# Prompt attention with its query tiles in falling order, and the next pair's projections moved to the short steps

## The reference

```
s = einsum('bqhr,bkr->bhqk', ql_b, ckv) + einsum('bqhd,bkd->bhqk', qr_b, kr)
s = where(pos[None, :] <= qp_b[:, None], s * ATTN_SCALE, NEG_INF)
p = softmax(s, axis=-1)
o = einsum('bhqk,bkr->bqhr', p, ckv)
```

## Time and profile before

| what | us |
|---|---|
| median of three runs | 2076.92 |
| the profiled execution | 2072.72 |
| its span, first to last instruction | 2070.9 |
| PE busy | 1934.8 |
| DVE busy | 1031.0 |
| ACT busy | 643.5 |

### The profile page before, as it was taken

One profiled execution on the slowest core, in us unless ns is written; L12 is line 12 of the kernel. 1 busy time (PEld: TensorE's weight loads), 2 busy tenths in 40 slices (PEclk: granted clock), 3 DMA queues, 4 the chain that ended last, 5 costly groups with the idle time before them and its releaser, 6 DMA issues. The chain is left out here.

```text
span 2070.9 us, 50992 instructions
## 1 busy us (share of the span) xinstructions
PE 1934.8 (93%) x22434; PEld 1248.1 (60%) x22434; DVE 1031.0 (50%) x2399; ACT 643.5 (31%) x1711; POOL 223.2 (11%) x223
## 2 busy tenths in 40 slices
PE   8999989988999999999989999899889999999997
PEld 5665667775566567754446656677755665677443
DVE  2017127775566468833330071277755664688333
ACT  1222234442455432310012222344424554322000
POOL 0000001010000034202100000001100000442022
PEclk9999999997999989999999999999979999999999
DMA  6102010000000367731121020100000002677121
GB/s 213 51 1 91 1 48 4 4 4 23 1 1 10 83 232 270 260 129 61 67 64 51 1 92 0 48 4 4 4 23 1 1 14 79 244 272 266 62 81 53
DMA packets 50112, 151.13 MB, mean 73 GB/s; under 512 B 15138, under 2 KB 19490, under 8 KB 40420
## 3 DMA queue, kind: packets, MB, share of 16 engines
q1 hardware_dynamic: 37604, 72.36, 10.5%
q0 software_dynamic: 12288, 75.51, 9.8%
HBM read 130.27 MB, written 12.86 MB: 69 GB/s over the span
## 5 line engine op out<-in xcount | busy, mean ns | idle before, releaser
L406 PE MATMUL psum<-work 128*128 128x368 f32 x1536 | 484.6, 476 | 8.9 <-DMA work<-w_z 6.6
L406 PEld LDWEIGHTS psum<-work 128*128 128x128 f32 x1536 | 293.6, 192 | 193.7 <-issue 8.2
L2465 PE MATMUL psum<-work,mixed 128*128 128x512 f32 (+1 forms) x576 | 248.8, 592 | 1.6 <-PEq L2137 1.6
L2465 PEld LDWEIGHTS psum<-work,mixed 128*128 128x128 f32 (+1 forms) x576 | 106.2, 186 | 137.7 <-issue 137.7
L2333 DVE STREAM_TRANSPOSE work<-work 128x1024 f32<-128x1024 f32 x128 | 150.5, 1214 | 0.3 <-issue 0.2
L1906 ACT ACTIVATE work<-psum,work 128x128 f32<-128x128 f32 (+8 forms) x130 | 98.0, 754 | 160.6 <-DVE work L2015 160.4
L1786 PE MATMUL psum<-work 96*128 96x512 f32 (+3 forms) x384 | 139.1, 495 | 2.3 <-ACT work L1906 2.1
L2077 POOL DMA_INDIRECT work<-cache_ckv,pages x64 | 60.7, 948 | 606.9 <-PE psum L1740 377.7
L2237 PE MATMUL psum<-work,ckv 128*64 128x256 f32 x1024 | 117.6, 382 | 0.7 <-ACT ckv L2292 0.7
L2513 DVE SCALAR_TENSOR_TENSOR work<-work,psum 128x512 f32<-128x512 f32 (+1 forms) x36 | 23.1, 683 | 162.1 <-PE psum L2465 162.1
L1786 PEld LDWEIGHTS psum<-work 96*128 96x128 f32 x384 | 67.4, 189 | 60.0 <-issue 43.5
(11 more groups left out here) (311 smaller groups left out, 2953.0 us busy)
## 6 DMA issues: line engine op xcount, KB each, us to landing
work<-w_z SPq DMA_DIRECT2D x4, 2560.0 KB, 11.0
work<-w_out SPq DMA_DIRECT2D x4, 2048.0 KB, 8.8
xres<-work SPq DMA_DIRECT2D x16, 512.0 KB, 2.9
work<-xT SPq DMA_DIRECT2D x4, 1104.0 KB, 8.8
work<-x_tok SPq DMA_DIRECT2D x8, 512.0 KB, 4.0
work<-xres SPq DMA_DIRECT2D x8, 512.0 KB, 4.3
work<-w_z SPq DMA_DIRECT2D x1, 2304.0 KB, 13.9
o_ckv<-ckv SPq DMA_DIRECT2D x2, 1104.0 KB, 4.3
```

Of the source, the lines that this page charges most:

```text
L406: return nc.tensor.matmul(zb[i % 2][n][:, 0:G], z_weights(m, g)[:, k, lo:lo + Z_W[i]], xT[:, k, span(n)], start=k == 0, stop=k == DK - 1)
L2465: last = nc.tensor.matmul(yb[t % 2][half][0:n, :], m.mixed[:, k, lo:lo + n], wo[half][:, k, :], start=k == 0, stop=k == DK - 1)
```

## The change

Two tables change; no instruction is added or taken away. `T_ORDER` becomes falling. The eleven pieces of the next pair, which stood in the slots 0 to 6 of a pair (none in slot 2, one in slot 3), now stand in the slots 2 to 7, with one per half slot but for the second half of slot 7. The `norm` pieces of the pair before move from slots 2 and 3 to both halves of slot 1.

```
-T_ORDER = [7, 0, 6, 1, 5, 2, 4, 3]
+T_ORDER = [7, 6, 5, 4, 3, 2, 1, 0]
...
-        PIECES += [(_s, 0, "q", _h, 0), (_s, 1, "q", _h, 1), (_s + 1, 0, "q", _h, 2), (_s + 1, 1, "lat", _h, 0),
...
+        PIECES += [(_s + 2, 0, "q", _h, 0), (_s + 2, 1, "q", _h, 1), (_s + 3, 0, "q", _h, 2),
...
-        PIECES += [(_s + 2, 0, "norm", _p - 1, 0), (_s + 3, 0, "norm", _p - 1, 1)]
+        PIECES += [(_s + 1, 0, "norm", _p - 1, 1), (_s + 1, 1, "norm", _p - 1, 0)]
```

More of the change, by code:

```diff
@@ L1603 @@
     if _p + 1 < PAIRS:
-        PIECES += [(_s, 0, "q", _h, 0), (_s, 1, "q", _h, 1), (_s + 1, 0, "q", _h, 2), (_s + 1, 1, "lat", _h, 0),
-                   (_s + 3, 1, "q", _h + 1, 0), (_s + 4, 0, "q", _h + 1, 1), (_s + 4, 1, "q", _h + 1, 2),
-                   (_s + 5, 0, "lat", _h + 1, 0), (_s + 5, 1, "k", _p + 1, 0), (_s + 6, 0, "k", _p + 1, 1),
-                   (_s + 6, 1, "k", _p + 1, 2)]
+        PIECES += [(_s + 2, 0, "q", _h, 0), (_s + 2, 1, "q", _h, 1), (_s + 3, 0, "q", _h, 2),
+                   (_s + 3, 1, "k", _p + 1, 0), (_s + 4, 0, "lat", _h, 0), (_s + 4, 1, "q", _h + 1, 0),
+                   (_s + 5, 0, "q", _h + 1, 1), (_s + 5, 1, "q", _h + 1, 2), (_s + 6, 0, "k", _p + 1, 1),
+                   (_s + 6, 1, "lat", _h + 1, 0), (_s + 7, 0, "k", _p + 1, 2)]
     if _p >= 1:
-        PIECES += [(_s + 2, 0, "norm", _p - 1, 0), (_s + 3, 0, "norm", _p - 1, 1)]
+        PIECES += [(_s + 1, 0, "norm", _p - 1, 1), (_s + 1, 1, "norm", _p - 1, 0)]
 PIECES += [(FIRST[PAIRS - 1] + 3, 1, "turn8", 0, 0), (N_STEP, 1, "norm", PAIRS - 1, 1),
```

## The result

The changed kernel takes 2087.02 us (median of five runs, 2085.25 to 2090.1), against 2076.92 for the kernel before: a ratio of 1.0038, 95% interval 1.002 to 1.0055. The forecast was 2080.2 with a range of 2074 to 2088. The medians differ by 10.1 us, which alone would be 1.0049; the ratio stands for 7.9 us and its interval for 4 to 11. So the sign of the sum was right and the size was not, since +3.3 was worked out. The measured time lies 1 us inside the upper end of the range.

The account below looks back on a forecast made before the run. PE's work was taken to bound the block, the order deciding only its idle time. Per layer -1.0 + 2 x 0.64 + 1.35 = +1.63, over two layers +3.3, added to the median: 2080.2 us, range 2074 to 2088.

Parts of the forecast that it names:

- +3.3: Both layers together: the forecast change in us, from a sum of waits of +1.63 a layer; bounds 0 and +8.
- What bounds the kernel: Attention block: PE's work is the block, and the order decides only over its idle time, some 5%.
- The interior pair: Interior pairs, twice a layer: new waits of 3.61 us against 2.97 before, +0.64 each.
- What would show it: Trace after: waits at `k`, `lat`, tile 7's, tile 6's and pair 3's first scores; a pair's period about 0.6 longer.
- Pair 0: First pair of a layer: waits of 3.9 us, including 1.2 for late ACT, against 4.9 before, so -1.0.
- Tail step and pair 3: End of a layer's block: waits of 5.05 us, including 2.3 behind the tail step, against 3.7 before, so +1.35.
- the guess for the last three steps: Last three steps, which have no pieces: 0.3 to 0.6 us at each of four handovers, 1.6 in all.
- its own last sign: Whole block: the prediction called itself wrong if the clock leaves 1.00 within the block.
- the one of the clock: Rival, pair 3's entry: the 2.3 us wait brings one clock fall in each layer, +13, 2093 us; chance 0.06.
- DVE did not become the bound: Rival, tiles 3 and 2: DVE becomes the bound, +1.5 us a pair, +9 in all, 2089; chance 0.14.
- That the short steps' waits don't arise: Rival, short steps: DVE and ACT drain pieces in time, -6.5 us a layer, -13 in all, 2064; chance 0.07.
- It does nothing: Rival, whole block: PE's work is the same and waits only change places, sum 0, 2077 us; chance 0.05.

Follow-up runs that it names:

- e1_fill: Changed kernel plus two needless matmuls between the tail step and pair 3's first scores; 2080.06 us, 1.0019 of the kernel before.
- e8_pair2_old_order: Changed kernel with pair 2 alone in the old order of tiles; 2082.7 us, 1.0021 of the kernel before.
- e4_spread: Falling order with the pieces spread: one in each of slots 0 to 2, two in 3 to 6, none in 7; 2070.72 us, 0.9963 of the kernel before.
- e5: e4_spread plus the needless matmuls of e1_fill at pair 3's entry; 2067.7 us, 0.9956 of the kernel before.
- e7: Kernel before with pair 2 alone in falling order, pieces as before; 2085.51 us, 1.004 of the kernel before.
- e2_order_alone: Kernel before with the falling order of tiles, pieces where they stood; 2087.89 us, 1.006 of the kernel before.
- e6: e4_spread with four transposes of pair 2's `norm` moved into the gap at pair 3's entry; 2069.86 us, 0.9958 of the kernel before.
- e3: Changed kernel with the old order of tiles, so only the pieces are moved; 2074.57 us, 0.9989 of the kernel before.

## Why the prediction was right and where it was wrong

**What bounds the kernel** was right in that PE's work is the block and no engine's work changed. It was wrong in that the order decides only over PE's idle time: behind the new wait the clock stretched the work itself, eight score rows from 3.67 to 6.71 us.

**The interior pair** was right in its three large terms, and by luck in its sum. Each wait is the idle time shown and 0.17, as in the prediction. `q` 0.20 + 0.17 = 0.37 (0.15 forecast), `k` 0.59 (0.49), `lat` 1.02 (1.07), the last `k` 0 (0.1), tile 7's scores 0.87 (0.9), tile 6's 0.72 (0.7), its second head 0 (0.2): 3.57 against 3.61. The small terms missed by +0.22, +0.10, -0.1 and -0.2, which cancel. The pairs' periods rose by 0.5 and 0.6 (0.64 forecast), and every wait named under "What would show it" is there in the rows.

**Pair 0** took 0.65 us longer, not 1.0 less, and yet its term held in sign and roughly in size. At pair 1's first scores the old order still has six transposes and twelve products more to do; the new one has done them by then, which by the prediction's spacing of 0.11 and of 0.055 for each of two rows is an estimated 2.0 us of work. So pair 0 won about 1.3 in waits, and the last part, which gets that work no more, lost 2.1 in e1_fill where it shows +0.1. The entry wait was 1.02 + 0.17 = 1.19; the 1.2 of the forecast was taken from another wait, with bounds of 0 and 2, so that hit is luck in part. The prediction's sum of pair 0's old waits, 4.05, goes with pair 1's first two waits (1.25 and 0.36 in pair 0) beside 1.28, 0.83 and 0.33, not with "the last two".

**Tail step and pair 3** were forecast at +1.35 and came to 2.1 without the fall. The tail step's wait (1.18 + 0.17 against 1.4) and that at pair 3's entry (2.12 + 0.17 against 2.3) came as worked out. Short was the guess for the last three steps: 0.76, 0.48 and 0.46 make with 0.51 a sum of 2.2, not 1.6. And the copies' wait of 0.65 is 0.85 where the clock holds (e1_fill), and disappears where it does not.

The sum of waits was +1.63 a layer by the prediction and +1.8 and +2.0 by e1_fill. That part of the forecast was a good one. That the whole time came inside the range, by 1 us, was luck: its upper end was set by longer `lat` and last-`k` waits and the spread of the runs, and those waits came as forecast, while the clock, which filled the room, had been left out of the sum. By its own last sign the forecast is wrong, since the clock left 1.00 within the block.

**The step that failed** is the one of the clock: "Against it: the waits of 1.3 us here leave the clock at 1.00. Chance 0.06." The kernel before shows waits of up to 1.3 us; the prediction itself worked out one of 2.3 and still let the small ones stand for it. The one fall that it had seen, at the sample block, argued the other way: an idle time of 1.28 us stands right ahead of it. Here is that place in the kernel before, and behind it the start of pair 0, where the 1.28 of the earlier trace rows lies:

```profile
743.00:752.00 9.00, 9.00 (x89) 6.81 (x97) 5.18 (x8) 2.23 (x10) 6.76 (x8) 0.50 0.95 332
530.00:545.00 15.00, 11.89 (x56) 7.11 (x56) 8.56 (x22) 5.95 (x18) 0.00 (x0) 1.00 0.00 1
```

So the same 1.28 us stood ahead of a fall in one place and of none in the other, and "1.3 us leave the clock at 1.00" was read from half of the rows. The rival's mechanism came in both layers; only its price was too high. It took over the 6.5 us of the sample block whole for each layer, 13 in all, while e1_fill gives 2.7 and 2.8, 5.5 in all: 6.8 us at half the clock lose 3.4, and 0.7 of it lies beside a wait that would have come anyway. Of the +9.3 in the blocks of the profiled executions, 3.8 are waits and 5.5 the clock. Had the prediction put this price on the likeliest case, it would have read 2080.2 + 5.5 = 2085.7.

The Trainium skill, TensorE: Matmul & The Clock Gate, section What's actually happening, says that the clock is set by how busy PE has lately been. Here that rule told against the change, and e1_fill agrees with it: matmuls that compute nothing of use keep the clock at 1.00 through the same 2.2 us. The Trainium skill, the same page, section A second HAM failure mode: psum-queue depth-cycling, has it that many short idle stretches between groups of matmuls can make the clock fall too. The rows of e8_pair2_old_order agree in kind only: there are two stretches, 0.55 and 1.23 us, close together.

**The other rivals.** DVE did not become the bound, though the condition that the prediction named (a rotation over 0.5 us behind its `q` piece) was met once: the rotation of 617.61 starts 1.07 us after the end of its piece, behind two row maxima, and that of 620.36 only 0.03. The next `q` piece waits 0.20 for it on PE, not 2 us, since PE's transposes and products lie between; so the sign of waits on `q` pieces came in small, and the price of 1.5 us a pair did not. That the short steps' waits don't arise was wrong for this placement of pieces, and right for that of e4_spread, where a pair takes 2.1 us less than before; the threshold that the prediction named, 1.5 us a pair, is passed there, and the kernel is faster. "It does nothing" fell with the interval, which lies above 1.

**What stays open**: what exactly makes the clock fall. Filling the gap at pair 3's entry takes the fall away there (e1, e5) and the short end of pair 2 brings it (e7); but the length of a single gap does not settle it, as the two of 1.28 us show. The 3.8 us outside the block in e2_order_alone are not explained either.

## What to carry to other kernels

Price a new wait twice, once as lost time and once as a gap behind which the engine may go on at half its clock. A few matmuls in the gap can pay even if nobody reads them: here they gave back 2.7 us a layer. An order from long to short brings all short steps together at the end of a group, and there the neighbours' chains lie open; small pieces of other work go where long steps cover their drain, not where PE has least to do; so spread (e4_spread), the falling order is faster than the old one. When the parts of a program are compared by their periods, look whether the cut between them moved: work that is done earlier makes one part longer and another shorter with no wait changed.

## What the runs showed of the hardware that was not expected

- A single idle gap of PE of 2.12 us (changed kernel, e2, e4, e7), and one of 1.54 (e6), stood ahead of 3.4 to 6.8 us at the lower clock. Gaps of 1.02 in pair 0 and 1.18 ahead of the tail step (changed kernel), 1.28 in pair 0, 1.38 behind pair 3's entry (e7, the first layer), 1.03 and 0.81 about that entry (e3), 0.82 and 0.64 (e1, e5) stood ahead of none. But 0.55 and 1.23 us close together (e8), and 1.28 ahead of the sample block, stood ahead of a fall.
- The same gap of 2.12 us gave 6.8 us at the lower clock in one layer and 3.4 in the other of one execution (e2, e4, e7), so its price cannot be read from one layer: e2's last part takes 62.5 us with 6.8 low and 61.6 with 3.4.
- A lower clock is no plain loss: of the 3.4 us that 6.8 us at half the clock lose here, 0.7 lay beside a wait.
